# Recurrence with odd chunks crossed and chunk products as four tiles; local y of chunks 8 to 16 inside the first steps of the state chain

## What is computed

```python
def step(S, inp):
    r_t, d_t, k_t, v_t, kk_t, a_t = inp
    sk = jnp.einsum('bhvk,bhk->bhv', S, kk_t)
    S = (S * d_t[:, :, None, :] - sk[..., None] * (kk_t * a_t)[:, :, None, :]
         + v_t[..., None] * k_t[:, :, None, :])
    return S, jnp.einsum('bhvk,bhk->bhv', S, r_t)
...
s_fin, ys = lax.scan(step, s0.astype(F32), (tm(r_h), tm(decay), tm(k_h), tm(v_h), tm(kk), tm(a_h)))
y = tm(ys)
mean = jnp.mean(y, axis=-1, keepdims=True)
var = jnp.mean(jnp.square(y - mean), axis=-1, keepdims=True)
y = ((y - mean) * lax.rsqrt(var + RW_GN_EPS)).reshape(b, t, d) * lnx_g + lnx_b
bonus = jnp.sum(r_h * k_h * r_k, axis=-1, keepdims=True) * v_h
y = (y + bonus.reshape(b, t, d)).astype(xn.dtype)
```

## Time and profile before

| | us |
|---|---|
| median of 3 runs | 4523.69 (4519.02 to 4526.64) |
| profiled execution, its own time | 4523.65 |
| its span | 4521.9 |
| TensorE busy | 4243.1 |
| VectorE busy | 1632.2 |
| ScalarE busy | 789.8 |
| recurrence, first chunk product to the last closing product | 782.3 |

### The profile page before, as it was taken

How to read it: one execution, slowest core, us unless ns; L and a number is a source line. 1 busy time by engine, 2 the same in 40 slices (tenths; PEclk the granted TensorE clock), 3 DMA queues, 4 the chain that set the end, 5 groups by cost and what they waited for, 6 DMA issues and landing times. The chain is left out here.

```text
span 4521.9 us, 76759 instructions
## 1 busy us (share of the span) xinstructions
PE 4243.1 (94%) x34224; PEld 2866.0 (63%) x34224; DVE 1632.2 (36%) x2684; ACT 789.8 (17%) x1893; POOL 143.9 (3%) x145
## 2 busy tenths in 40 slices
PE   5999799999989999999997999999937999999998
PEld 2566588888866666666565666666625666666556
DVE  6000377666533433332012235454532433333001
ACT  1000222222102111111011222222212211111000
POOL 0000000000001000000000000000000100000001
PEclk8999899999889999999998999999968999999999
DMA  1122200011020111111222111111054011111223
GB/s 62 54 71 77 67 26 26 30 33 34 9 100 1 39 34 39 39 35 61 102 102 82 46 35 46 45 35 46 32 209 185 24 39 35 39 39 33 106 99 129
DMA packets 85444, 264.73 MB, mean 59 GB/s; under 512 B 37000, under 2 KB 43528, under 8 KB 76552
## 3 DMA queue, kind: packets, MB, share of 16 engines
q1 hardware_dynamic: 85128, 259.96, 16.6%
HBM read 224.34 MB, written 35.58 MB: 57 GB/s over the span
## 5 line engine op out<-in xcount | busy, mean ns | idle before, releaser
L279 PE MATMUL ps<-sb_h,sb_w 128*128 128x384 f32 (+1 forms) x4224 | 1289.8, 468 | 1.8 <-issue 1.8
L279 PEld LDWEIGHTS ps<-sb_h,sb_w 128*128 128x128 f32 x4224 | 801.7, 190 | 485.2 <-issue 2.8
L311 PE MATMUL ps<-sb_big,sb_w 128*128 128x384 f32 (+1 forms) x2112 | 646.6, 468 | 1.2 <-ACT sb_tmp L398 1.2
L1461 PE MATMUL ps<-sb_h,sb_w 128*128 128x384 f32 (+1 forms) x1728 | 575.8, 479 | 16.1 <-DMA sb_tmp<-c_amask 13.6
L311 PEld LDWEIGHTS ps<-sb_big,sb_w 128*128 128x128 f32 x2112 | 400.2, 190 | 241.6 <-ACT sb_tmp L398 2.2
L1461 PEld LDWEIGHTS ps<-sb_h,sb_w 128*128 128x128 f32 x1728 | 315.9, 192 | 197.9 <-issue 29.4
L486 DVE COPY sb_tmp<-sb_tmp 128x2 f32<-128x2 f32 x88 | 14.9, 169 | 760.9 <-ACT sb_tmp L398 760.9
L620 PE MATMUL ps<-sb_big,sb_w 128*128 128x384 f32 (+1 forms) x768 | 234.5, 468 | 0.0
L417 DVE TENSOR_TENSOR sb_tmp<-sb_tmp 128x384 f32<-128x384 f32 (+1 forms) x63 | 34.8, 552 | 526.4 <-ACT sb_tmp L343 524.7
L395 ACT ACTIVATE sb_tmp<-ps 128x384 f32<-128x384 f32 x176 | 86.2, 490 | 731.8 <-PE ps L279 731.8
L620 PEld LDWEIGHTS ps<-sb_big,sb_w 128*128 128x128 f32 x768 | 145.8, 190 | 88.5 <-issue 0.5
(11 more groups left out here) (244 smaller groups left out, 4151.6 us busy)
## 6 DMA issues: line engine op xcount, KB each, us to landing
sb_w<-wdown SPq DMA_DIRECT2D x46, 1408.0 KB, 6.0
sb_w<-wup SPq DMA_DIRECT2D x88, 512.0 KB, 3.6
sb_w<-wqkv SPq DMA_DIRECT2D x36, 512.0 KB, 3.6
sb_big<-kT SPq DMA_DIRECT2D x8, 2304.0 KB, 13.9
sb_big<-vc SPq DMA_DIRECT2D x8, 2304.0 KB, 15.6
rkv_scratch<-sb_w SPq DMA_DIRECT2D x24, 544.0 KB, 2.7
...
```

What stands on the lines that cost most here:

```text
L279: mm = pe.matmul(m.ps[:, 3 * q + b, 0:n], wt[f % 2][q][:, k, :], m.H[:, k, t0:t0 + n], start=(k == 0), stop=(k == KT - 1))
L311: mm = pe.matmul(m.ps[:, u % 6, 0:n], wdt[u % 2][:, f, :], hid[:, f, t0:t0 + n], start=(f == 0), stop=(f == FT - 1))
L1461: mm = pe.matmul(m.ps[:, ring(s, p), 0:w], wt[t][:, k, :], m.H[:, k, t0:t0 + w], start=(k == 0), stop=(k == KT - 1))
```

## The change

It does the following, all in `rwkv_core`:

- Of odd chunks, the results of most stages are stored crossed: head 0 on partitions 64 to 127 and head 1 on 0 to 63 (`side`). `chunks` takes for each stage whether its operands and its results are `plain` or `crossed`; where these differ, an odd chunk's products go from rows 0-63 to columns 64-127 and back. Chunks go two at a time, so four products in a row use four different tiles; even and odd chunks go to different banks.
- A stage is cut in two halves (chunks 0-7 and 8-16) of two banks each, with one signal per half. Three pairs of banks rotate in place of two sets of three banks. VectorE and ScalarE take 8 chunks with one instruction, and chunk 16 with one of its own.
- `Yc` is no longer updated on VectorE in each level. A stage `z` turns `Xc` into it on TensorE, and ScalarE copies it; only `y5` still goes through VectorE. The subtraction that began `Yc` is gone too. ScalarE also takes `H`. `E` and `N` skip the sample chunk.
- The local part of `Y` of chunks 0 to 7 stays ahead of the chain. That of chunks 8 to 15 is made in steps 1 to 4 of the chain (`y_local`), the sample's terms in step 5 (`y_samples`). The gates move to steps 2, 4 and 6 and share one pair of banks, with each other and with the output gate.

```diff
@@ -648,29 +647,40 @@
     PIPE = [(0, "sa"), (0, "kn"), (0, "bonus"), (1, "sa")]
     for i in range(PAIRS):
         PIPE += [(i, "at"), (i, "kq")] + ([(i - 1, "mean")] if i else []) + [(i, "rb"), (i, "rk"), (i, "bt"), (i, "kt"), (i, "vt")]
-        PIPE += ([(i - 1, "vn")] if i else []) + [(i, "qt"), (i, "bv"), (i, "t0"), (i, "t1"), (i, "x1"), (i, "y1"), (i, "t2"),
-                                                  (i, "x2"), (i, "y2")]
-        PIPE += ([(i + 1, "kn")] if i < LAST else []) + [(i, "t3"), (i, "x3"), (i, "y3")]
-        PIPE += ([(i + 1, "bonus")] if i < LAST else []) + [(i, "t4"), (i, "x4"), (i, "y4"), (i, "t5"), (i, "y5"), (i, "G"),
-                                                            (i, "H"), (i, "E"), (i, "N"), (i, "RP"), (i, "Y")]
+        PIPE += ([(i - 1, "vn")] if i else []) + [(i, "qt"), (i, "bv"), (i, "t0"), (i, "t1"), (i, "z0"), (i, "x1"), (i, "t2"),
+                                                  (i, "z1"), (i, "x2")]
+        PIPE += ([(i + 1, "kn")] if i < LAST else []) + [(i, "t3"), (i, "z2"), (i, "x3")]
+        PIPE += ([(i + 1, "bonus")] if i < LAST else []) + [(i, "t4"), (i, "z3"), (i, "x4"), (i, "t5"), (i, "z4"), (i, "y5"),
+                                                            (i, "G"), (i, "H"), (i, "E"), (i, "N"), (i, "RP"), (i, "Y")]
         PIPE += ([(i + 2, "sa")] if i + 2 < PAIRS else []) + [(i, "g")]
     PIPE += [(LAST, "mean"), (LAST, "vn")]
-    BY_ACT = {"sa", "g", "bt", "kt", "vt", "qt", "bv", "G"}
-    SLOT, BEFORE, FULL, TAKEN = {}, {}, {}, {}
-    slot, last, counts = 1, {}, {"d": 0, "a": 0, "y": 0, "full": 0}
-    for n, (i, st) in enumerate(PIPE):
-        prev = PIPE[n - 1][1] if n else None
-        if not (st == "g" and prev == "sa" or st == "at"):
-            slot = 1 - slot
-        SLOT[i, st] = slot
-        BEFORE[i, st] = last.get(slot)
-        last[slot] = (i, st)
-        who = "y" if st == "Y" else "a" if st in BY_ACT else "d"
-        TAKEN[i, st] = (who, counts[who])
-        counts[who] += 6 if st == "sa" else 3
-        if st != "Y":
-            FULL[i, st] = counts["full"]
-            counts["full"] += 3
+    BY_ACT = {"sa", "g", "bt", "kt", "vt", "qt", "bv", "z0", "z1", "z2", "z3", "z4", "G", "H"}
+    PAIR, BEFORE, FULL, TAKEN = {}, {}, {}, {}
+    recent, users, counts = [0, 1, 2], {}, {"d": 0, "a": 0, "y": 0, "full": 0}
+    in_chain = None
+    for i, st in PIPE:
+        for half in range(3 if st == "sa" else 2):
+            if st == "at" and half == 0 and in_chain is not None:
+                recent, in_chain = [in_chain[0], in_chain[2], in_chain[1]], None
+            if st in ("sa", "g") and in_chain is not None:
+                p = in_chain[2]
+            else:
+                p = recent.pop(0)
+                recent.append(p)
+            if st == "Y" and half == 1:
+                in_chain = (PAIR[i, "Y", 0], p, recent[0])
+            u = (i, st, half)
+            PAIR[u] = p
+            BEFORE[u] = users.get(p)
+            users[p] = u
+            who = "y" if st == "Y" else "a" if st in BY_ACT else "d"
+            counts[who] += 1
+            TAKEN[u] = (who, counts[who])
+            if st != "Y":
+                counts["full"] += 1
+                FULL[u] = counts["full"]
+        if st == "g" and i == LAST:
...
-                for g, (c0, c1) in enumerate(G3):
-                    wait_taken(pool, i, "at", g)
+                for half, (c0, c1) in enumerate(((0, 8), (8, NCH))):
+                    wait_taken(pool, i, "at", half)
                     pool.tensor_tensor(AMc[:, c0:c1, :], ATc[:, c0:c1, :], bc(lm[:, 0, :], c1 - c0), ALU.mult).then_inc(am, 1)
...
                 for g, (t0, n) in enumerate(TB):
                     wait_full(act, i, "sa", g)
                     for q, (dst, bias) in enumerate(((SG, PW0), (A, PA0))):
-                        act.activation(dst[:, t0:t0 + n], both(i, 2 * g + q), ACT.Sigmoid, bias=col(i, bias)).then_inc(outa, 1)
-
-            def out_gate(i, g):
-                t0, n = TB[g]
-                wait_full(act, i, "g", g)
-                act.activation(G[:, t0:t0 + n], flat(i, "g", g), ACT.Copy).then_inc(outa, 1)
+                        ins = act.activation(dst[:, t0:t0 + n], m.ps[:, 2 * PAIR[i, "sa", g] + q, 0:n], ACT.Sigmoid, bias=col(i, bias))
+                    ins.then_inc(outa, 1)
+
+            def out_gate(i, half):
+                wait_full(act, i, "g", half)
+                act.activation(flat(G, half), flat_ps(i, "g", half), ACT.Copy).then_inc(outa, 1)
...
             def out(i, st, dst, scale=1.0):
-                for g, (c0, c1) in enumerate(G3):
-                    wait_full(act, i, st, g)
-                    act.activation(dst[:, c0:c1, :], bank(i, st, g), ACT.Copy, scale=scale).then_inc(outa, 1)
-
-            def take_y(i, g):
-                t0, n = TB[g]
-                act.wait_ge(yfull, 3 * i + g + 1)
-                act.activation(YT[:, t0:t0 + n], flat(i, "Y", g), ACT.Copy).then_inc(ytaken, 1)
+                wait_full(act, i, st, 0)
+                act.activation(octet(dst, 0), octet_ps(i, st, 0), ACT.Copy, scale=scale).then_inc(outa, 1)
+                wait_full(act, i, st, 1)
+                act.activation(octet(dst, 1), octet_ps(i, st, 1), ACT.Copy, scale=scale)
+                act.activation(dst[:, SC, :], sample_psum(i, st), ACT.Copy, scale=scale).then_inc(outa, 1)
+
+            def take_y(i, half):
+                act.wait_ge(yfull, 2 * i + half + 1)
+                ins = act.activation(octet(ch(YT), half), octet_ps(i, "Y", half), ACT.Copy)
+                if half:
+                    ins = act.activation(ch(YT)[:, SC, :], sample_psum(i, "Y"), ACT.Copy)
+                ins.then_inc(ytaken, 1)
...
                 out(i, "bv", BVc)
+                out(i, "z0", Yc)
                 if ahead:
                     roots(ahead)
+                out(i, "z1", Yc)
                 if ahead:
                     powers(ahead)
+                out(i, "z2", Yc)
+                out(i, "z3", Yc)
                 if ahead:
                     inverse_powers(ahead)
+                out(i, "z4", Yc)
                 out(i, "G", Gc, scale=-1.0)
+                out(i, "H", Hc)
                 act.wait_ge(small_ps, SUMS[i, "U"])
                 act.activation(Us, m.ps[:, 7, 0:HD], ACT.Copy, scale=-1.0).then_inc(acts, 1)
                 if i + 2 < PAIRS:
...
             def mask(i, st, which, dst):
-                for g, (c0, c1) in enumerate(G3):
-                    wait_full(dve, i, st, g)
-                    for s0, s1, sampled in split(g):
-                        ins = dve.tensor_tensor(dst[:, s0:s1, :], bank(i, st, g, s0 - c0, s1 - c0),
-                                                bc(ms[:, which + 2 * sampled, :], s1 - s0), ALU.mult)
+                for half in range(2):
+                    wait_full(dve, i, st, half)
+                    ins = dve.tensor_tensor(octet(dst, half), octet_ps(i, st, half), bc2(ms[:, which, :]), ALU.mult)
+                    if half:
+                        ins = dve.tensor_tensor(dst[:, SC, :], sample_psum(i, st), ms[:, which + 2, :], ALU.mult)
                     ins.then_inc(outd, 1)
...
+            def from_one(i, st, dst):
+                for half in range(2):
+                    wait_full(dve, i, st, half)
+                    ins = dve.tensor_tensor(octet(dst, half), bc2(two), octet_ps(i, st, half), ALU.subtract)
+                    if half and st == "t0":
+                        ins = dve.tensor_tensor(dst[:, SC, :], two, sample_psum(i, st), ALU.subtract)
+                    ins.then_inc(outd, 1)
...
+                for l in range(1, 6):
+                    if l == 3 and ahead:
+                        unit_keys(ahead)
+                    if l == 4 and ahead:
+                        bonuses(ahead)
+                    level(i, l)
+                    if l == 1 and ahead:
+                        inverse_norms(ahead)
+                    if l < 5:
+                        update(i, f"x{l}", Xc)
...
             def gates(i, g):
 
                 t0, n = TB[g]
                 pe.wait_ge(ld_w, 16 * (i + 1))
-                for q in (2 * g, 2 * g + 1):
-                    if q >= 3:
-                        wait_taken(pe, i, "sa", q - 3)
-                    elif BEFORE[i, "sa"] is not None:
-                        wait_taken(pe, *BEFORE[i, "sa"], q)
+                free(i, "sa", g)
+                p = 2 * PAIR[i, "sa", g]
                 for c in heads:
                     for q, r in enumerate(heads):
-                        mm = pe.matmul(both(i, 2 * g + q)[c], lw[r, q, c], lora[r, 0, t0:t0 + n], start=True, stop=True)
+                        mm = pe.matmul(m.ps[c, p + q, 0:n], lw[r, q, c], lora[r, 0, t0:t0 + n], start=True, stop=True)
                 mm.then_inc(full, 1)
 
-            def out_gate(i, g, part):
...
+            def side(h, c, kind):
+
+                return heads[h ^ (c % 2 if kind == "crossed" else 0)]
...
```

(62 more changed lines are left out.)

293 lines of the change are left out of this document (132 added, 161 removed).

## The result

The changed kernel takes **4479.78 us** (median of 4, 4465.98 to 4483.5), the kernel before 4524.67: a ratio of 0.990, 95% interval [0.989, 0.991]. That is faster, but by 45 us and not by 120. The profiled execution took 4479.17 us, its span is 4477.4.

A forecast was written before the change was run, and what follows sets the result against it. TensorE's matmuls were taken to set the pace before the chain, VectorE next, 17 us below. Savings of 152 us less 32 for the clock gave 120, so 4404 us (own range 4380 to 4432); full range 4365 to 4480.

The forecast's parts named there:

- The rate of four tiles: Chunk products on four 64 x 64 tiles: 14.6 ns a record, with bounds of 13.9 and 29.2 (no gain).
- Rival C: Chunk products: the four tiles don't overlap, 29.2 ns a record, +1.1 us a pair, 4532 us; chance 0.06.
- instruction blocks: Instruction delivery in the recurrence: 16 KB blocks lasting 1.9 us each cost 0, at most 3 us a pair.
- S2: Inversion levels of a head pair: 33.6 us before, forecast 26.4, so 7.2 us go.
- S3: Products G to Y of a head pair: 16.8 us before, forecast 10.0, so 6.8 us go.
- The loop of 4.44 us a level: Inversion levels: halves passing between TensorE, ScalarE and VectorE bind at 4.44 us, against TensorE's own 3.15.
- S1: Chunk products up to the level masks: 28.6 us before, forecast 22.2 with VectorE as bound, so 6.4 us go.
- The chain: State chain ending each pair, 17.1 us before: +2.4 us with gates (pairs 0 to 5), +0.8 elsewhere.
- The clock: TensorE's lower clock level over the recurrence: four cold chains of eight and a short fall per pair, net cost 32 us.
- Rival A: Chunk products: crossed tiles overlap only partly or instruction blocks come too slowly, 22 ns a record, 4456 us; chance 0.12.
- Rival B: Recurrence: four tiles work, but half the pairs stay at 1.2 GHz through the levels, all chains too; 4484 us; chance 0.15.
- Rival D: Recurrence: slower by the clock alone, 782 us reached with 54% at the lower level; 4577 us at 0.65; chance 0.04.

## Why the prediction was right in part and wrong in size

- **The rate of four tiles was right.** 124 products from 769.13 take 2.03 us less 0.22 of drain, 14.7 ns each; I had 14.6. Rival C (no overlap) is out, and so is the reading of the Trainium skill (TensorE: Matmul & The Clock Gate, Part 3) by which a load is held behind products in flight in its own rows: 64 x 64 tiles that share rows ran at this rate. Nor was its floor of about 25 ns from start to start seen inside a block.
- **The step that failed is the one on instruction blocks**: "at 14.6 ns a block lasts 1.9 us. No row shows blocks that close: I charge 0, and up to 3 us a pair as the upper bound". The waits for issue are 9.3 us a pair, 66 us of them ahead of the chains, where 91 were missing. My bound had no row behind it. The kernel before has 12 blocks in the 50.4 us of S2 and S3, 4.2 us apart, and no two in its whole trace start closer than 3.37 us; I was asking for 1.9. The bound should have been 3.37 us a block, 26.3 ns a product. By it S3's 467 products take 12.3 us where I had 10.0, and they took 13.0. What was left of S3's gain is hardly more than its 116 products fewer: 583 to 467 by 28.9 ns is 3.4 us, and it was 3.9.
- **S2** was 32.8 us in pair 2 where I had 26.4. The loop of 4.44 us a level was right, and it bound: level 4, which met no block's end, took 4.45 us, from the first of these lines to the last, with the waits for ScalarE and VectorE in it that the loop has:

```profile
750.86 1.39 PE L1263 MATMUL ps<-sb_big 64*64 64x64 f32 x66
...
753.60 1.46 PE L1263 MATMUL ps<-sb_w 64*64 64x64 f32 x68 [0.24 <-ACT sb_w L886]
755.31 1.43 PE L1263 MATMUL ps<-sb_big 64*64 64x64 f32 x61 [0.25 <-DVE sb_big L1064]
```

Levels 1 to 3 took 5.12, 5.50 and 4.87 us, of which 0.74, 1.07 and 0.47 are waits for issue: 4.38, 4.43 and 4.40 without them. So the blocks' ends came on top of the loop, 4.6 us in this S2 and 3.3 on average. The other 1.8 us are sizes: the last level took 6.25 us without its waits for issue where I had 5.2, key norms and bonus 4.25 for 3.5. The new stage z puts as many products on TensorE as the updates of Yc had, and there is one such stage more (1102 products in S2 for 1028); what taking the updates from VectorE is worth by itself, no run measures.
- **S3** took 13.0 for 10.0.
- **S1** took 23.6 at the upper clock for 22.2, VectorE busy for 89% of it; this step held best. Over the pairs 0 to 6 it still gave 26.6 us for 47.4. Of these 21 us some 8 are the same 1.4 in six pairs, 5 are pair 0 (20.1 us for 14.9, with 2.4 of waits for issue), and the rest lies in the five pairs in whose S1 the clock was at the lower level for 4 to 7 us (24.1 to 26.2 us).

The loop is built from copies that came out as said, 688 ns for a half on VectorE where I had 0.69 us and 598 ns on ScalarE where I had 0.60. By form in the changed kernel, 620 to 1237 us (columns as in the earlier trace rows):

```profile
L1056 DVE TENSOR_TENSOR sb_w<-ps,sb_tmp 128x512 f32<-128x512 f32 x70 | 46.7, 688 | 15.7 <-PE ps L1263 15.1
L886 ACT ACTIVATE sb_w<-ps 128x512 f32<-128x512 f32 x55 | 32.9, 598 | 163.6 <-PE ps L1263 163.6
```

- **The chain** was right: 19.4 us at the upper clock for 17.1 + 2.4, with waits of 1.43 and 0.90 where I had 1.4 and 1.0.
- **The clock**'s net cost of 32 us was about right, in part by luck. Three chains were cold where I had four: of the 33 us that the chains grew by, 14 are the 2.3 that each of the six with gates grew at the upper clock, which leaves some 19 for the clock where I had 28. Outside the chains I had one short fall in each pair; there were 16 stretches of the lower clock, 66 us, for 7 and 26 us before. At my 1.5 us a fall the 9 more are 14 us where I had 4, an estimate that no run here tests. Over the recurrence the granted clock was 0.91, just outside the 0.75 to 0.9 that I had named. The mechanism was only half seen. I took the products in the chain as a load on it; they also help to keep its clock: with local y ahead of the chain the kernel took 4531.
- **Rival A** named this cause, "or instruction blocks come too slowly", and priced it at halfway, 22 ns. With 28.9 ns in S2 and S3 its sum is 4.9 + 1.8 + 3.3 - 2.4 = 7.6 us a pair, 61 in all, less 32 for the clock: 4495, within 15 of the result. Its price, not its place, was off. Rival B's time (4484) is that of the result, but its mechanism isn't: no pair stayed at the lower clock through the levels. That the result lies inside my range, 0.2 us below its end of 4480, is luck: the end was drawn for A and B, not for the forecast's own terms. Rival D has a slip that nothing else rests on: it takes the part of the recurrence's work that is done at the lower level for the part of the time, so its 54% and 70% go with granted means of 0.68 and 0.61 and not of 0.73 and 0.65.
